# Mixed attention of a two-layer block: the next head's query and key rounding and remainders placed two to three steps sooner, with the loads reordered head by head

## What is computed

```
def hybrid_layer(x, ...):
    h = rms_norm_2(x, attn_norm_w)
    proj = h @ w_in
    ret_cols, dsa_cols, dil_cols = jnp.split(proj, ...)
    mixed = jnp.concatenate([retention_mixer(...),      # 4 heads
                             dsa_mixer(...),            # 4 heads, 256 chosen keys per query
                             dilated_mixer(dil_cols)],  # 8 heads, three dilated patterns
                            axis=-1)
    x = x + mixed @ w_out
    h = rms_norm_2(x, mlp_norm_w)
    return x + jnp.square(jax.nn.relu(h @ w_up)) @ w_down
```

## Time and profile before

| | us |
|---|---|
| median of 3 runs | 3043.29 |
| lowest, highest | 3041.71, 3046.94 |
| the profiled execution | 3047.4 |
| its span in the trace | 3045.6 |
| PE busy in the span | 2686.6 |
| DVE busy | 1819.3 |
| ACT busy | 1255.0 |

### The profile page before, as it was taken

The page is one execution under the profiler, slowest core; times in us unless marked ns, Lnnn a source line. Parts: engine busy times, 40 slices in busy tenths (PEclk is TensorE's granted clock), DMA queues, the critical chain, the costliest instruction groups (busy, mean ns, idle before and its releaser), DMA issues.

```text
span 3045.6 us, 32610 instructions
## 1 busy us (share of the span) xinstructions
PE 2686.6 (88%) x11872; PEld 2048.7 (67%) x11872; DVE 1819.3 (60%) x2758; ACT 1255.0 (41%) x1746; POOL 160.8 (5%) x197
## 2 busy tenths in 40 slices
PE   5689989899887399999399978999989997999998
PEld 1468566666676287888386746788868674678886
DVE  5643157677675599999636666444443666644444
ACT  5423235444432277777433254322223325432222
POOL 0011000000000111111101000000000100000000
PEclk9799999999998699999689979999999997999999
DMA  9457324443441399999423242222222324222222
GB/s 320 140 154 208 92 62 124 122 111 92 142 166 69 124 364 374 372 361 350 143 78 114 84 134 74 83 96 91 88 79 78 111 86 130 78 83 91 88 96 76
DMA packets 238009, 436.36 MB, mean 143 GB/s; under 512 B 71568, under 2 KB 94368, under 8 KB 237887
## 3 DMA queue, kind: packets, MB, share of 16 engines
q1 hardware_dynamic: 220335, 391.71, 39.6%
q0 software_dynamic: 17552, 43.05, 4.2%
HBM read 399.84 MB, written 50.58 MB: 148 GB/s over the span
## 4 chain that ended last, share of the span: by engine, by line
PE 52%; DVE 14%; ACT 5%; DMA 4%; issue 4%; POOL 1%; DVEq 0%; SPq 0%; ACTq 0%; POOLq 0%
PE BKP L788 36%; DVE WL L2600 2%; PE BKP L1023 1%; PE BKP L1194 1%; PE BKP L1197 1%; PE BKP L1196 1%; DVE G L2240 1%; DMA W<-in_w_expert_gu_dram 1%; ACT WH L1719 1%; DVE hL L2600 1%; DMA G<-in_w_expert_gu_dram 1%; PE SCP L1194 1%; PE SCP L1196 1%; PE SCP L1197 1%; PE SCP L1276 1%
## 5 line engine op out<-in xcount | busy, mean ns | idle before, releaser
L1935 DVE TENSOR_TENSOR WL<-W,WH 128x2048 fp32r<-128x2048 f32 x130 | 297.9, 2292 | 479.8 <-ACT WH L1341 478.3
L1341 ACT ACTIVATE WH<-W 128x2048 fp32r<-128x2048 f32 x130 | 248.7, 1914 | 606.8 <-PE BKP L788 542.5
L788 PE MATMUL BKP<-hH,WH 128*128 128x512 f32 x896 | 356.2, 398 | 8.0 <-DVE hL L2377 5.9
L788 PE MATMUL BKP<-hH,WL 128*128 128x512 f32 x896 | 351.8, 393 | 0.0
L788 PE MATMUL BKP<-hL,WH 128*128 128x512 f32 x896 | 351.6, 392 | 0.0
L788 PE MATMUL BKP<-WH,aH 128*128 128x512 f32 (+1 forms) x544 | 215.1, 395 | 22.8 <-DVE aL L2580 10.7
L788 PE MATMUL BKP<-WL,aH 128*128 128x512 f32 (+1 forms) x544 | 211.2, 388 | 0.0
L788 PE MATMUL BKP<-WH,aL 128*128 128x512 f32 (+1 forms) x544 | 211.0, 388 | 0.0
L788 PE MATMUL BKP<-WH,hH 128*128 128x512 f32 (+3 forms) x512 | 201.8, 394 | 6.9 <-ACT Z L1392 2.7
L788 PEld LDWEIGHTS BKP<-hH,WH 128*128 128x128 f32 x896 | 170.8, 191 | 49.1 <-issue 10.4
L788 PEld LDWEIGHTS BKP<-hL,WH 128*128 128x128 f32 x896 | 170.0, 190 | 36.2
(11 more groups left out here) (492 smaller groups left out, 5678.6 us busy)
## 6 DMA issues: line engine op xcount, KB each, us to landing
W<-in_w_expert_gu_dram SPq DMA_DIRECT2D x46, 1024.0 KB, 7.7
G<-in_w_expert_gu_dram SPq DMA_DIRECT2D x46, 1024.0 KB, 7.6
W<-in_w_in_dram SPq DMA_DIRECT2D x42, 1024.0 KB, 5.3
W<-in_w_up_dram SPq DMA_DIRECT2D x32, 1024.0 KB, 5.2
W<-in_w_down_dram SPq DMA_DIRECT2D x32, 1024.0 KB, 5.1
W<-in_w_expert_down_dram SPq DMA_DIRECT2D x24, 1024.0 KB, 6.3
G<-in_w_expert_down_dram SPq DMA_DIRECT2D x22, 1024.0 KB, 7.3
X<-in_w_in_dram SPq DMA_DIRECT2D x16, 1024.0 KB, 8.7
```

What stands on the lines that cost most here:

```text
L788: mm = pe.matmul(BK[j][:, 0:cols], lt, rh, start=start and a == 0, stop=stop and a == len(q) - 1, skip_group_check=True)
L1341: act.activation(WH[s][:], W[s][:] if raw is None else raw, ACT.Copy).then_inc(sems["w_hi"], 1)
L1935: v.tensor_tensor(WL[s][:], W[s][:] if raw is None else raw, WH[s][:].bitcast(F32), ALU.subtract).then_inc(sems["w_lo"], 1)
```

## The change

ACT rounds a head's queries and keys at tt = 2 of the head that used the slot before, two steps ahead of where it stood. DVE takes the remainders at tt = 3 (at n = 0 of body 0 for head 5). Head 5 is rounded before the loop, in `first_head(3)`. SP's list becomes one of scores' loads and values' loads in turn, head by head.

```
--- before.py
+++ after.py
@@ mixed_heads (SP)
+                def scores_of(h):
+                    sp.wait_ge(sems["head_lo"], T.next("head_lo"))
+                    sp.sem_inc(sems["paused"], 1)
+                    qk(h, h % 2)
+                scores_of(6)
+                scores_of(7)
+                weights_in()
+
                 def later(i):
                     for s in range(2):
-                        sp.wait_ge(sems["head_lo"], T.next("head_lo"))
-                        sp.sem_inc(sems["paused"], 1)
-                        qk(i * 2 + (6 + s), s)
-                    if i == 0:
-                        weights_in()
-                    for s in range(2):
+                        if i < 4:
+                            scores_of(i * 2 + (8 + s))
                         sp.wait_ge(sems["head_o"], T.next("head_o"))
                         sp.sem_inc(sems["paused"], 1)
                         values(i * 2 + (6 + s), s)
@@ mixed_attention, body (ACT)
-                        if tt == 0 and not (last and s == 1):
-                            mixed_rounded(1 - s, l)
+                        if tt == 2 and not last:
+                            mixed_rounded(s, l)
@@ first_head (ACT)
                         mixed_rounded(0, l)
+                    if j == 3:
+                        mixed_rounded(1, l)
@@ mixed_attention, body (DVE)
+                        if first and n == 0:
+                            mixed_remainders(1, l)
                         if first:
                             beside(n)
-                        if tt == 1 and not (last and s == 1):
-                            mixed_remainders(1 - s, l)
+                        if tt == 3 and not last:
+                            mixed_remainders(s, l)
```

## The result

The changed kernel is slower, as forecast:

| | before | changed |
|---|---|---|
| median of 6 runs | 3045.88 | 3064.38 |
| lowest, highest | 3041.71, 3049.95 | 3057.08, 3066.82 |
| profiled execution, its span | 3047.4, 3045.6 | 3066.82, 3065.0 |

What follows compares the result with a forecast made beforehand. PE was taken to bound bodies 3 and 4, DVE body 0, DVE and ACT in turn body 1. Loops +8.2 and entries +4.4 made +12.6 us: 3060.0 profiled, 3055.9 median, range 3047 to 3063.

Steps and rivals of the forecast that it cites:

- The entry: Before the loop, head 5's rounding waits for loads ahead of bank copy 3, delaying first scores: +2.0 and +2.4 us.
- The step that chose 3.0 us for the landing: At the entry, head 5's last load lands 3.0 us after issue, chosen between 2.7 and 4.5 in the rows.
- Body 0: DVE bounds it and gets three pairs of remainders instead of two, so body 1's first `top` comes +1.31 us later.
- Body 1: DVE and ACT wait for each other in turn; gains and losses of moved roundings and remainders by step sum to -0.3 us.
- The term for step 3: In body 1, DVE's remainders moved to step 3 cost 1.31 us less the 0.48 that DVE waited: +0.8.
- Body 2: Roundings ahead of `output` and remainders ahead of `put_rest` delay PE in step 3: +1.4 us; second half +0.2.
- some 2 us in each run: Rival, slower by more: PE's clock falls in body 2 for 3 to 4 us of PE work, 3060; chance 0.08.
- Bodies 3 and 4: Roundings between exponential and copy find 0.35 us slack for 1.04: +0.7 first half, +0.2 second, +0.9 for each body.
- Body 5: One rounding and one pair of remainders fewer at steps 0 and 1: -0.3 us.
- Faster: Rival: the remainder waits were on PE's path, so removing them gives 3027.7, or 3037.7 for half; chance 0.07.
- No difference: Rival: slack is larger by half, the loops come out even and only the entry costs +4.4, 3047.7; chance 0.15.
- Late loads: Within the slower rival: head loads reach ACT late at step 2, 1.6 us each, +16 in all; rival's chance 0.08.

Runs made afterwards that it cites:

- E2: The kernel before with only head 5's rounding moved in front of bank copy 3; loads, later roundings and remainders as before: 3051.56, ratio 1.0016.
- E6: The kernel before with the new loads and ACT's roundings at tt = 2; head 5 and all remainders as before: 3050.92, ratio 1.0010.
- E4: The changed kernel with eleven unread 128 x 512 products on PE in body 2, ahead of the product that waits for `put_rest`: 3058.95, ratio 1.0036.
- E3: The changed kernel with ACT's step 2 roundings behind the copy and `output`, and DVE's step 3 remainders behind `put_rest`: 3057.18, ratio 1.0039.
- E5: The kernel before with the new order of the loads alone, roundings and remainders as before: 3044.87, ratio 0.9993.
- E7: The kernel before with new loads, roundings at the end of step tt = 3 behind the copy, remainders next step behind `top`: 3041.85, ratio 0.9980.
- E1: The changed kernel with head 5 rounded and its remainders taken in body 0 as before: 3059.76, ratio 1.0040.
- E10: The changed kernel with the loads in the order of the kernel before: 3103.00, ratio 1.0187.
- E9: E7 with unread 128 x 128 products on PE, five in each of body 1's steps 5 to 7, ten in body 2's wait: 3038.53, ratio 0.9970.
- E8: The kernel before with unread 128 x 128 products on PE in body 0, five steps of body 1 and body 2's wait: 3044.76, ratio 0.9988.

## Why the prediction was right, and where it was off

Of the 19.1 us in the loops of the profiled execution the forecast has the entries (4.4 predicted, 4.5 measured) and bodies 3 to 5 (3.0 and 2.9). It is short by 4.3 us in body 2 (3.2 and 7.5) and by 2.1 in bodies 0 and 1 (2.0 and 4.1). The order of the instructions was read rightly in the main; both shortfalls are the clock of PE, which the sum had at nothing.

**The entry: right.** +2.0 and +2.4 predicted, +2.02 and +2.51 in the profile, and E2 has them alone. The step that chose 3.0 us for the landing holds: from the issue at 2522.84 to ACT's start at 2525.98 it is 3.1, between the 2.7 and the 4.5 of the earlier trace rows. The Trainium skill's fit (DMA: Bandwidth & Descriptors, Anatomy of one DMA), an estimated 2.3 us, was measured for transfers that POOL issues, and is too short for these, which SP issues. Its rule for kernel authors in the same page, to issue early and wait late, is what this place breaks, and the trace agrees with it: ACT waits 8.20 us there.

**Body 0: right, though the table hides it.** Three pairs of remainders on DVE instead of two were to bring body 1's first `top` +1.31 us later; the table has +0.75 and +0.58. Its mark is the start of PE's values, and the last pair runs behind that mark. The `top` that the prediction speaks of, first before, then changed:

```profile
2538.38 0.42 DVE L2260 CUSTOM_DVE_ANT_0 W<-BKP,G 128x256 f32<-128x256 f32 x1 [0.33 <-DVE BIG L2769]
...
2549.95 0.42 DVE L2266 CUSTOM_DVE_ANT_0 W<-BKP,G 128x256 f32<-128x256 f32 x1
```

From the first scores it is 20.80 us before (2517.58 to 2538.38) and 22.09 in the changed kernel (2527.86 to 2549.95): +1.29 in layer 1, and +1.30 in layer 0. The whole pair counts.

**Body 1: right in layer 0 with body 0** (+1.0 predicted for the two, +1.06 measured), **off by 2.1 us in layer 1** (+3.07). The term for step 3, +0.8 for the remainders, is the +0.86 of the second half in both layers; E6, without their move, has 0.00 there. From body 1's first `top` to body 2's, layer 0 takes 26.27 us before and 26.30 in the changed kernel, against the -0.3 of the sum. The windows of the changed kernel show the cause in layer 1: the values that open body 1 run at 0.50 until almost 2554. In layer 0 of the same execution they run at 1.00, and the half body takes 13.35 us instead of 15.39. E4, whose instructions are the same up to there, has 0.50 for 1.3 us in layer 1 and takes 13.52. So it is not the order that makes this part of the loss in that execution but the moment at which the clock rises, which the same instructions reach differently each time. Whether it is also why runs of one kernel spread, 9.7 us for the changed one and 8.2 for before in as many runs, is not shown. No run shows which of the short waits in body 0 decides it; that stays open. So how much of these 2.1 us an average run has is open too.

**Body 2: the step that was mis-sized.** "So +1.04 + 0.4 = **+1.4**" is right for the chain: 1.45 and 1.48 by E3 and E4, and PE's wait grew by 1.43. The sum left out that PE at rest for 3.15 us comes back at the lower clock. That is +1.5 us in layer 0 by E4, for 3.4 us at 0.50. The prediction had it only in a rival ("some 2 us in each run", 0.08), with the mechanism right and the chance far too low. In layer 1 the changed kernel's body 2 takes 3.84 more than E4's: 3.06 in the first half and 0.78 in the second, into which the low clock reaches. It also starts the body with 2.0 us more at 0.50, some 0.9 by the 0.46 above; an estimated 2.9 is left for the low clock behind the wait, which lasts 6.2 us from PE's restart (2.8 by the 0.46). With 1.5 and 2.9 added the sum would have been +17.0, within the interval of 13 to 20. That the clock falls behind such a wait is no accident of one execution. In the twelve loops of before, E2, E3, E5 and E7, and of E4 with its filler, PE waits 0.67 to 1.73 us at this place and the clock stays at 1.00. In the eight of the changed kernel, E1, E6 and E10 it waits 2.75 us or more, and each time the clock is at 0.50 behind it, for 2.9 to 6.2 us of PE's work.

**Bodies 3 and 4: right.** +0.7 and +0.2 predicted, +0.70 and +0.17 measured, in both layers and both bodies. The chain that ended last, in body 3 of the changed kernel (start, us on the chain, engine, output, line), shows the stretch with no slack:

```profile
2607.47 0.81 ACT AT L1593 x2
2608.29 0.52 ACT WH L1585
2608.81 0.52 ACT WH L1586
2609.33 0.37 ACT W L1630
2609.70 0.52 ACT hH L1598
2610.23 0.38 ACT AT L1593 x2
2610.61 0.49 ACT W L1630
2611.10 0.04 issue
2611.14 1.07 PE BKP L1027 x2
```

From the exponential of step 3 to the values there is no gap on ACT, and both roundings, 1.04 us, lie in it; 0.70 of them reach PE. E6 shows that ACT's move alone does it.

**Body 5: right**, -0.3 against -0.30 and -0.27.

**The rivals.** *Faster* is ruled out as a whole: 15.1 us of waits for remainders vanished, and the loop got longer. But a part of it was there to be had: E7, which takes the same work off body 1's steps at another place, is 4.6 us shorter there in the two runs. *No difference* failed on the slack, which was as small as counted. *Late loads* did not happen, since the new order prevents it; E10 shows what they would have cost.

## What to carry to other kernels

The size of a wait in a table of waits is not its worth: look at what the engine does right behind it, and whether another queue lets that start sooner. When small work is moved on an engine that works in order, first find the stretch in which no other engine waits for it (here behind the copy that releases the values, beside 2.4 us of PE work), and never put it in front of the instruction that the bound engine waits for, above all not if it waits for a transfer itself. Where a wait of PE grows, count the low clock behind it, too: here 1.7 us went unpunished, and 2.5 us (E10), 2.75 (E6) and 3.15 did not. Idle products in such a wait can prevent it (E4); with too many of them the product that ends the wait starts late.

## What the runs showed of the hardware

- PE at rest for 3.15 us came back at 0.50 of full clock, which lasted 3.4 us in layer 0, and cost 1.5 us there against E4, and 6.8 us in layer 1. After 2.75 us the clock was at 0.50 within 0.4 us of PE's restart, for 3.4 us in both layers (E6); after 2.54 and 2.67 us in bodies 3 and 4 of E10 it was there for 3.4 and 6.8 us. After a wait of 1.72 us in the same place as the first the clock stayed at 1.00 (E3).
- The same instructions meet a different clock in each execution and layer: at the start of body 2 the kernels here, those without idle products, had between 1.9 and 5.2 us at 0.50, and E3's two layers differ by 1.48 us for that alone, 0.46 us for each microsecond of low clock.
- Idle products of 128 x 128 brought the clock of the DVE-bound body 0 from 0.75 to 0.90 and made the body 0.7 us longer; in body 2's wait ten and twelve of them put the waiting product 0.26 and 0.47 us later (E9, E8), and E4's eleven of 128 x 512, in a longer wait, did not delay it.
